# A hybrid decoder step on one core: where the sample group's work and the dense filler stand in the engines' order

## The reference

```
mod = silu(c) @ w_ada + b_ada                       # 6 vectors: shift, scale, gate, twice
h = rmsnorm(x) * (1 + sc1) + sh1
proj = h @ w_in                                     # HGRN2, Mamba-2 and RWKV-7 inputs
o_hg  = HGRN2 recurrence   (4 heads, 64x64 state per head)
o_mb  = Mamba-2 recurrence (8 heads, 64x64 state per head, causal convolution before it)
o_rw  = RWKV-7 recurrence  (4 heads, 64x64 state per head)
x = x + g1 * (concat(o_hg * silu(g), norm(o_mb * silu(z)), o_rw) @ w_out)
h = rmsnorm(x) * (1 + sc2) + sh2
x = x + g2 * ((silu(h @ w_gate) * (h @ w_up)) @ w_down)
y = rmsnorm(x);  outputs: y and the new states of both groups
```

## Time and profile before

| | |
|---|---|
| median of the runs | 2077.51 us (2077.34 to 2079.49) |
| profiled execution | 2070.94 us, span 2069.2 us, mean granted clock 0.882 |
| stage 1 | blocks 0 to 7 from 175.3 us; last prompt step 666.0 us; stage ends 733.5 us |
| stage 2, blocks 0 to 2 | 766.0 to 903.5 us |
| stage 2, blocks 3 to 7 | 903.5 to 1300 us |
| stage 2, samples, `x`, rest of the filler | 1300 to 1484.1 us |
| stage 3 | from 1484.1 us to the end |

### The profile page before, as it was taken

One profiled execution on the slowest core, in us unless ns is written; L12 is line 12 of the kernel. 1 busy time (PEld: TensorE's weight loads), 2 busy tenths in 40 slices (PEclk: granted clock), 3 DMA queues, 4 the chain that ended last, 5 costly groups with the idle time before them and its releaser, 6 DMA issues.

```text
span 2069.2 us, 31916 instructions
## 1 busy us (share of the span) xinstructions
PE 1685.7 (81%) x13471; PEld 1527.3 (74%) x13471; DVE 963.5 (47%) x2087; ACT 592.1 (29%) x1057; POOL 289.0 (14%) x348
## 2 busy tenths in 40 slices
PE   4998887888766827767688788678897999999996
PEld 2898776877644813346677677678787999999995
DVE  6314456754343454455545453555554243333434
ACT  3224222322221432223333342324333212222222
POOL 3501001110000220013333333300000000000000
PEclk9999888988866866759799899889998999999998
DMA  7111001110100234512122212333232132131311
GB/s 287 46 41 31 22 25 38 45 29 23 33 1 1 84 128 142 166 56 68 54 68 68 83 57 77 115 114 114 84 102 61 49 95 74 59 89 47 107 41 56
DMA packets 199013, 149.22 MB, mean 72 GB/s; under 512 B 6447, under 2 KB 187168, under 8 KB 197592
## 3 DMA queue, kind: packets, MB, share of 16 engines
q1 hardware_dynamic: 188482, 120.67, 19.3%
q0 software_dynamic: 7440, 23.27, 3.3%
q10 hardware_dynamic: 2950, 3.24, 0.4%
HBM read 134.03 MB, written 13.18 MB: 71 GB/s over the span
## 4 chain that ended last, share of the span: by engine, by line
PE 67%; DVE 19%; ACT 6%; DMA 4%; issue 3%; POOL 0%; SPq 0%; POOLq 0%; DVEq 0%; ACTq 0%
PE bank L1183 17%; PE bank L1184 16%; PE bank L1185 16%; PE bank L1122 2%; DMA RAW<-in_w_ada 2%; PE bank L1191 1%; PE bank L1551 1%; PE bank L1552 1%; PE bank L1370 1%; PE bank L1371 1%; PE bank L1319 1%; ACT WHI L1690 1%; PE bank L1381 1%; PE bank L1326 1%; PE bank L1328 1%
## 5 line engine op out<-in xcount | busy, mean ns | idle before, releaser
L1690 ACT CAST WHI<-RAW 128x1024 fp32r<-128x1024 f32 (+4 forms) x210 | 187.9, 897 | 346.7 <-PE bank L1185 343.1
L1183 PE MATMUL bank<-HBH,WHI 128*128 128x328 f32 (+1 forms) x832 | 261.1, 314 | 14.3 <-DVE HBL L2235 10.1
L1184 PE MATMUL bank<-HBL,WHI 128*128 128x328 f32 (+1 forms) x832 | 259.6, 312 | 0.0
L1185 PE MATMUL bank<-HBH,WLO 128*128 128x328 f32 (+1 forms) x832 | 258.8, 311 | 0.0
L2118 DVE TENSOR_TENSOR WLO<-RAW,WHI 128x1024 fp32r<-128x1024 f32 (+4 forms) x131 | 134.5, 1030 | 231.4 <-ACT WHI L1690 231.0
L944 POOL TENSOR_TENSOR WLO<-RAW,WHI 128x1024 fp32r<-128x1024 f32 (+1 forms) x79 | 165.7, 2099 | 512.0 <-ACT WHI L1690 512.0
L1183 PE MATMUL bank<-HHI,WHI 128*128 128x344 f32 x624 | 213.4, 342 | 18.3 <-ACT STG L1722 7.0
L1184 PE MATMUL bank<-HLO,WHI 128*128 128x344 f32 x624 | 205.9, 330 | 0.0
L1185 PE MATMUL bank<-HHI,WLO 128*128 128x344 f32 x624 | 205.2, 329 | 0.0
L1183 PE MATMUL bank<-HAH,WHI 128*128 128x384 f32 x416 | 151.8, 365 | 56.6 <-DVE HAL L2235 16.4
L1183 PEld LDWEIGHTS bank<-HBH,WHI 128*128 128x128 f32 x832 | 157.1, 189 | 15.5 <-issue 15.3
(11 more groups left out here) (500 smaller groups left out, 3110.6 us busy)
## 6 DMA issues: line engine op xcount, KB each, us to landing
RAW<-in_w_gate SPq DMA_DIRECT2D x44, 512.0 KB, 3.9
RAW<-in_w_up SPq DMA_DIRECT2D x44, 512.0 KB, 3.9
RAW<-in_w_ada SPq DMA_DIRECT2D x32, 512.0 KB, 4.7
RAW<-in_w_in SPq DMA_DIRECT2D x26, 512.0 KB, 3.8
ADAW<-in_w_ada SPq DMA_DIRECT2D x8, 1024.0 KB, 19.5
RAW<-in_w_out SPq DMA_DIRECT2D x16, 512.0 KB, 4.2
RAW<-in_w_down SPq DMA_DIRECT2D x32, 256.0 KB, 2.8
RAW<-in_w_down SPq DMA_DIRECT2D x16, 384.0 KB, 3.4
```

The costliest lines, as they stand in the source:

```text
L1183: mm(bank[:, 0:w], whi[:, k, :], hi_k, start=(k == 0), stop=False)
L1184: mm(bank[:, 0:w], whi[:, k, :], lo_k, start=False, stop=False)
L1185: last = mm(bank[:, 0:w], wlo[:, k, :], hi_k, start=False, stop=(k == nk - 1))
L1690: a.copy(w_split(i)[0][:, 0:nk, :], RAW[u % NRAW][:, 0:nk, :]).then_inc(w_hi, 1)
```

## The change

1. **Samples.** The steps `rws(1)` to `rws(3)`, `smp_tok`, `smp_state` and `smp_out` are cut into 32 items (`SAMPLES`). One follows each step of blocks 0 to 2 of stage 2 (but `mb_out`). On PE they write one bank, 2, in turns: a user waits until the last one's reader is done (`S_READ`). They have tiles of their own. The first RWKV steps of the samples (mixing, gates) join those of prompt block 7, with `rws0` on PE.
2. **silu.** The 18 pieces stand behind `rw_lin`, `rw_inv2`, `rw_lora` and `rw_inv3` of blocks 3 to 7; `hgg` is projected before `xbc` so that its tiles are there.
3. **Filler of stage 1.** `TAIL` is gone; quanta 67 to 77 stand in blocks 5 to 7.
4. **Banks.** The dense quanta of stage 2 take turns on three banks (2, 3, 7). Mamba-2's second decay half and its norm use banks 4 and 0 instead of 7, so `hg_att` waits for `mb`'s scale.
5. **Filler of stage 2.** `FILL` has six places of two halves, one whole quantum each. A `pause` ends a filling early: ahead of the first `down` of a group and between the steps of the norm after `w_out`.

```
-        TAIL = [1, 8, 1, 0]
+        silu = list(range(3 * 6))
...
         for item in rw_list:
             PLAN1.append(item)
-            fill(min(BEHIND.get(item[0][3:], 0), len(left) - left_in_tail))
-        for st in range(4):
-            PLAN1.append(('rws', st))
...
+            if item == ('rw_gates', NB - 1):
+                PLAN1.append(('rws0', 0))
+            fill1(BEHIND.get(item[0][3:], 0))
+            if item[0] in ('rw_lin', 'rw_inv2', 'rw_lora', 'rw_inv3') and silu and (
+                    item[1] >= (4 if item[0] in ('rw_lin', 'rw_lora') else 3)):
+                PLAN1.append(('silu', silu.pop(0)))
...
+        PLAN1.append(('rw_final', 0))
...
-            b = 3 if q < QP2 else 2 + (q - QP2) % 2 if q < QP2A else q % 7
+            b = 3 if q < QP2 else (2, 3, 7)[(q - QP2) % 3] if q < QP2A else q % 7
...
             if q == LASTQ[N1 + 7]:
-                ffn += [('ev', q), ('sum', 3), ('scaled', 3), ('rest', 3)]
+                ffn += [('ev', q), ('sum', 3), ('pause', 0), ('scaled', 3), ('pause', 0), ('rest', 3), ('pause', 0)]
...
-        FILL = {'hg_att': 2, 'hg_state': 1, 'mb_decay': 3, 'hg_o': 2, 'mb_prod': 3, 'hg_sq': 2, 'mb_turn': 2, 'mb_sq': 2,
-                'hg_levels': 2, 'mb_out': 1}
+        SAMPLES = ['sr1', 'sh1', 'sm1', 'sh2', 'sm2', 'sr2', 'sr3', 'sh3', 'sr4', 'sh4', 'sm3', 'sr5', 'sh5', 'sr6', 'sr7',
+                   'sr8', 'sh6', 'sh7', 'sr9', 'sm4', 'sm5', 'sh8', 'sr10', 'sm6', 'sr11', 'sh9', 'sm7', 'sr12', 'sh10',
+                   'sr13', 'sm8', 'sm9']
+        samples = list(SAMPLES)
+        FILL = {'hg_att': 2, 'mb_decay': 2, 'hg_o': 2, 'mb_prod': 2, 'mb_turn': 2, 'hg_levels': 2}
...
                 PLAN2.append(item)
+                if samples and item[0] != 'mb_out':
+                    PLAN2.append((samples.pop(0), 0))
...
-        PLAN2.append(('smp_tok', 0))
-        fill(6)
         PLAN2.append(('mix_final', 0))
-        fill(4)
-        PLAN2.append(('smp_state', 0))
-        fill(8)
-        PLAN2.append(('smp_out', 0))
-        fill(4)
         for i in range(3, 9):
             PLAN2.append(('x', i))
-            fill(2)
+            fill(3)
+        samples_at = len(PLAN2)
         PLAN2.append(('mark', 0))
-        fill(8)
+        fill(10, True)
...
                 elif what == 'mix_final':
+                    pool.wait_ge(hg_dve, step(HG_DVE, 'out', NB - 1))
+                    load_x(12, XTOK3)
+                    load_x(13, XTOK3)
...
+                if what in S_USERS[1:]:
+                    pe.wait_ge(*S_READ[S_USERS.index(what) - 1][1])
...
+                elif what == 'sh6':
+                    pe.wait_ge(*hs_at('dve')('opart'))
+                    mm(S[0:32, 0:64], G4[:, :], SO[:, :], start=True, stop=True).then_inc(hs_pe, 1)
```

More of the change, by code:

```diff
@@ L126, in dense_plan @@
     rw = [('rw', t) for t in range(7)] + [('dt', 0)]
-    mb = [('z', t) for t in range(4)] + [('xbc', t) for t in range(6)]
-    hg = [('hgg', t) for t in range(2)] + [('hg', t) for t in range(6)]
+    mb = [('z', t) for t in range(4)] + [('hgg', t) for t in range(2)] + [('xbc', t) for t in range(6)]
+    hg = [('hg', t) for t in range(6)]
     units = rw + mb + hg + ada
@@ L411, in kernel_program @@
         AEX = r2.t("AEX", [P, 8])
[L414 to L417, removed]
         XTOK3 = [hw.t(f"XTOK3_{i}", [P, D]) for i in range(2)]
-        SSM = mw.t("SSM", [P, 2048])
-        SMT = mw.t("SMT", [P, 2048])
+        w1 = Region(h_end, mix_end - 4 * KT * T)
+        SSM = w1.t("SSM", [P, 2048])
+        smt_at = w1.at
+        SMT = w1.t("SMT", [P, 2048])
+        SWK = Region(h_end, w1.at).t("SWK", [P, 1024])
+        SW1 = Region(smt_at, w1.at).t("SW1", [P, 1024])
         r2b = Region(mix_end, hi)
@@ L429, in kernel_program @@
         XTOK2 = [ha.t(f"XTOK2_{i}", [P, D]) for i in range(2)]
-        PSG = [ha.t(f"PSG{i}", [P, T]) for i in range(2)]
         ADT2 = ha.t("ADT2", [P, 512])
+        SHG = ha.t("SHG", [P, 1024])
+        SHT2 = ha.t("SHT2", [P, 1024])
+        STK = ha.t("STK", [NS, 1024])
+        SWV = ha.t("SWV", [P, 336])
+        sf_at = r2b.at
         SGF = [r2b.t(f"SGF{i}", [P, FCW[0]]) for i in range(2)]
@@ L718, in kernel_program, with fill1 @@
         BEHIND = {'turn': 1, 'lin': 1, 'gates': 1, 'inv4': 1, 'post': 1, 'decay': 2}
[L719 to L722 removed]
+        silu = list(range(3 * 6))
+        def fill1(n):
             for _ in range(n):
@@ L732, in kernel_program @@
             PLAN1.append(item)
-            fill(min(BEHIND.get(item[0][3:], 0), len(left) - left_in_tail))
-        for st in range(4):
-            PLAN1.append(('rws', st))
-            if st == 0:
-                PLAN1.append(('rw_final', 0))
-            if st == 1:
-                fill(3)
-                PLAN1 += [('silu', i) for i in range(3 * 6)]
-                fill(TAIL[1] - 3)
-            else:
-                fill(TAIL[st])
-        assert not left
+            if item == ('rw_gates', NB - 1):
[4 more added lines that the diff above has]
+                PLAN1.append(('silu', silu.pop(0)))
+        assert not silu
+        fill1(len(left))
         PLAN1.append(('ev', QP1 - 1))
+        PLAN1.append(('rw_final', 0))
         PLAN2 = [('pre', 0), ('hg_logits', 0), ('mb_turn', 0), ('hg_gate', 0), ('hg_levels', 0)]
         late = list(range(QP1, QP2))
-        ffn = [('mixsplit', 0), ('split', n1s)]
+        ffn = [('mixsplit', 0), ('split', n1s), ('pause', 0)]
+        up_ends = [u for u in range(N1, N2 - 1) if UNITS[u][0] == 'up' and UNITS[u + 1][0] == 'down']
         for q in range(QP2, QP2A):
@@ L1435, in _ @@
                     rw(what[3:], arg)
-                elif what == 'rws':
-                    rws(arg)
+                elif what == 'rws0':
+                    rws0()
                 elif what == 'rw_final':
```

820 lines of the change are left out of this document (459 added, 361 removed).

## The result

The changed kernel takes 1989.36 us (median of 4 runs, 1983.74 to 1995.37) against 2078.03 us for the kernel before in the same session: a ratio of 0.9573 (95% interval 0.9543 to 0.9602), 88.7 us less. Forecast were 2020 us, range 1985 to 2055. The profiled execution took 1990.94 us.

A forecast was written before the change was run, and what follows sets the result against it. The kernel was taken as bound by PE where dense quanta stand back to back, by chains between engines elsewhere. Terms -54 + 28 + 35 - 139.5 + 73 = -57.5 took 2070.94 to 2013.4, plus 6.6 gave 2020 us, range 1985 to 2055.

The forecast's parts named there:

- rival 1: Chains hide more: blocks 3 to 7 at the floor of 225, blocks 0 to 2 less; about 1978 us, chance 0.22.
- End of stage 1, -54: Last prompt step to stage 2: 67.5 us shrink to 13.5 with `rw_final` alone left, saving 54.
- Blocks of stage 1, +28: Stage 1's blocks grow by 28 us: ten quanta 13 and 3 more, silu 5 and 3, `rws0` about 4.
- The silu term: Stage 1's blocks: 18 pieces at 0.3 us each, 5, and 3 more for changing ACT's tables twice.
- Blocks 0 to 2, +35: Stage 2: nearly the full DVE time of the samples' work lengthens these blocks, by 35 us; block 1 most, to about 70.
- strict reading of shared DMA engines: Blocks 0 to 2 of stage 2: states' transfers delay `w_ada` loads, a bound of 38 us; the forecast took nothing.
- Blocks 3 to 7, -139.5: Stage 2: with less filler, 225 us of PE work plus 32 idle make 257, against 396.5 before.
- Behind the blocks, +73: After stage 2's blocks: filler that left them lengthens this stretch from 184.1 to 257 us.
- Stage 3, 0: Stage 3: the change does not touch it, so no difference.
- From profile to median, +6.6: Whole kernel: the runs' median lies 6.6 us above the profiled execution, so 2013.4 becomes 2020.
- Rival 2: Blocks 3 to 7 run slower when sparse, at clock 0.67 in place of 0.93: +33, about 2053 us, chance 0.17.
- Rival 3: Stage 2: the samples' one bank stops PE, 16 items at 4.15 us make 66; 2086 us, chance 0.06.

The follow-up runs named there:

- experiment 6: The changed kernel with ten dense quanta kept for the end of stage 1 again: 2018.35 us, ratio 0.9701.
- experiment 2: The changed kernel with all 18 silu pieces in one lump behind stage 1's last eviction: 2006.06 us, ratio 0.9665.
- experiment 4: The kernel before with only the filler's new table (12 halves at six places in place of 22 at ten): 2054.78 us, ratio 0.9894.
- experiment 7: The changed kernel with the last `up` product evicted behind the next split again, without the pause ahead of `down`: 2010.35 us, ratio 0.9672.

## Why the prediction was right, and where its sizes were off

The signs held, and so did the main mechanism: the stage's end loses the samples' chain, the blocks of stage 2 lose filler, and less than that comes back behind them. The size was off. The time, 1989.36 us, lies outside the 2000 to 2040 to which I gave 0.53, nearer to rival 1's 1978, and 4 us inside the wide range. The traces differ by 80.0 us, I had 57.5. The 22.5 us between them are these terms of the sum:

- **End of stage 1, -54.** It was -54.7, and 12.7 us from the last prompt step to POOL's release where I had 13.5.
- **Blocks of stage 1, +28, measured +20.4.** Nine quanta in blocks 5 and 6 (215 of PE's products) cost 10.2 us, 1.1 each (experiment 6), where I had 13 and 3 more for ten. The silu term, 5 and 3 for the tables, was wrong: spread silu cost nothing (experiment 2). Block 6 is 6.4 us longer than before even without filler (62.1 us in experiment 6 against 55.7). `rws0` and the samples' mixing and gates stand there, for which I had 4. The 4 us left were not measured alone.
- **Blocks 0 to 2, +35, measured +29.6.** This is near by luck. I took the full DVE time of the passes, 29.6 us, and 5 for small operations; leaving the passes out gave back 15.7. The other 14 are nearly all in block 1, and in my sum they have 5 for small operations and nothing for the clock. Without the passes block 1 still ran at 0.64 where it had been 0.79, with PE busy some 8 us longer. PE also waited 4.16 us for one `w_ada` tile there, where the longest such wait before was 2.20. How the 14 divide between clock, hand-overs, small operations and transfers wasn't measured. Block 1, forecast at 70, took 70.5. The 38 us that the strict reading of shared DMA engines would give did not come; 1 of the 4 MB, though, is loaded from 708.5 us on, ahead of block 0.
- **Blocks 3 to 7, -139.5, measured -133.3.** 263.2 us where I had 257, with PE busy 221.1 where I had a floor of 225. The idle time was 8.4 us a block, not 6.5.
- **Behind the blocks, +73, measured +56.9.** The largest error, in two steps. First, from quantum 166 on I took 7 us for the samples' last steps and 4 for six `x` off the 113.7 us. Experiment 4, which has the old banks and the old order there, took 93.5: so it was 20, not 11. Second, I kept three transitions to `down` at 3.5 us and took as unchanged those behind quantum 166. The change evicts the last `up` product ahead of the next split, and from quantum 166 on they cost 1.94 (experiment 7). Banks and order together brought the 93.5 down to 87.4. I had read that edit in the difference of the plans and given it no price.
- **Stage 3, 0:** +1.1, of the size of the spread.
- **From profile to median, +6.6.** The profiled execution of before was 6.6 us below its median. After, it was 1.6 above. That is the other 8 us of the miss: one profiled run is one draw from a spread of 12 us (of the four of the changed kernel), and its distance to the median doesn't carry over.

The rivals. The chains did hide more, in blocks 0 to 2 (15.7 us of the passes were on the path, not 29.6) and a little by the price of a quantum, but blocks 3 to 7 stayed 38 us above the floor that rival 1 gave. Rival 2 did not decide where it was priced: blocks 3 to 7 ran at a clock of 0.87, as the filled blocks of stage 1 had, and not at 0.67. The Trainium skill's rule ("TensorE: Matmul & The Clock Gate", § HAM oscillation — how this bites in real kernels) fits blocks 0 to 2 (0.72, 0.62, 0.60) and not those with a whole quantum at six places. In block 1, at 0.62 to 0.64, the low clock is part of what my sum had left out. Rival 3 fell: in blocks 0 to 2 of the changed kernel all of PE's waits above 2 us are for `w_ada` tiles (up to 2.37), for ACT's part of the Mamba-2 norm (3.38 and 3.51) and the two shown for DVE's passes.

## What to carry to other kernels

Price work that moves into another engine's idle time by what stands behind it in that engine's queue, not by how idle the engine is: the same nine passes cost PE a wait of 11.5 us ahead of a 0.30 us copy that freed a bank for the product at the head of PE's queue, and one of 5.2 us behind it. When a change puts an eviction ahead of a weight's split, price it at each place where it occurs: at the last places it was 1.6 us, in block 6 it was 6. And when two executions are compared, take the same step in both as the mark, and read the granted clock beside the length: block 7 of stage 1 took 43.8 us at 0.80 and 50.6 at 0.52.
